# Turning the keys of a unit by 64x64 products with the identity, behind the values, in a two-layer decoder trunk on one core

## What is computed

```
def rwkv7_scan(r, w, k, v, kk, a):        # 16 heads of 64 channels
    def step(state, inp):
        rt, wt, kt, vt, kkt, at = inp
        sa = jnp.einsum("bhvk,bhk->bhv", state, -kkt)
        state = (state * wt[:, :, None, :] + sa[..., None] * (kkt * at)[:, :, None, :]
                 + vt[..., None] * kt[:, :, None, :])
        return state, jnp.einsum("bhvk,bhk->bhv", state, rt)
...
    xx = token_shift(h) - h
    xm = h[None] + xx[None] * mu.astype(F32)[:, None, None, :]
    rkvz = jnp.einsum("pbtd,pde->pbte", xm[:4], w_rkvz)
```

## Time and profile before

| | before |
|---|---|
| median of 3 runs | 3664.91 us |
| lowest, highest | 3661.26, 3670.25 us |
| the profiled execution | 3667.72 us |
| its span, first to last instruction | 3665.9 us |
| mean granted TensorE clock | 0.951 of full |
| TensorE busy | 3335.7 us, 91% |
| VectorE busy | 1609.7 us, 44% |
| ScalarE busy | 1316.8 us, 36% |
| GpSimd busy | 223.1 us, 6% |
| chain that ended last | TensorE 76%, VectorE 11%, DMA 5%, ScalarE 4% |

### The profile page before, as it was taken

The page is one execution under the profiler, slowest core; times in us unless marked ns, Lnnn a source line. Parts: engine busy times, 40 slices in busy tenths (PEclk is TensorE's granted clock), DMA queues, the critical chain, the costliest instruction groups (busy, mean ns, idle before and its releaser), DMA issues.

```text
span 3665.9 us, 76910 instructions
## 1 busy us (share of the span) xinstructions
PE 3335.7 (91%) x33546; PEld 2023.8 (55%) x33546; DVE 1609.7 (44%) x3443; ACT 1316.8 (36%) x2492; POOL 223.1 (6%) x345
## 2 busy tenths in 40 slices
PE   2898998899889858999999999999999999999998
PEld 1555465456446534666656466656556656556663
DVE  7254254335434534444554244454334454334442
ACT  0343243334333334333443233443324354323332
POOL 0010001010001000000000000000000000000000
PEclk8999999999999988999989999989999999999999
DMA  7231322223133121112011211111121111121111
GB/s 322 70 94 50 111 83 82 76 70 88 70 93 108 56 93 31 43 38 67 25 43 60 76 44 60 37 37 54 42 78 42 60 38 33 58 88 38 42 50 51
DMA packets 275847, 247.30 MB, mean 67 GB/s; under 512 B 16252, under 2 KB 251960, under 8 KB 272952
## 3 DMA queue, kind: packets, MB, share of 16 engines
q1 hardware_dynamic: 273208, 233.99, 20.2%
q0 software_dynamic: 2304, 8.39, 0.6%
HBM read 217.17 MB, written 25.18 MB: 66 GB/s over the span
## 4 chain that ended last, share of the span: by engine, by line
PE 76%; DVE 11%; DMA 5%; ACT 4%; issue 2%; SPq 1%; DVEq 0%; ACTq 0%; POOL 0%; another core or an unknown queue 0%
PE bank L655 20%; PE bank L529 14%; PE bank L624 6%; PE bank L739 4%; PE bank L752 4%; PE bank L562 3%; PE bank L748 3%; PE bank L526 3%; DVE xm L1534 3%; PE bank L604 3%; DVE arena L1595 2%; PE bank L666 2%; DMA xm<-in_ada_w 2%; PE bank L794 1%; DMA arena<-residual_scratch 1%
## 5 line engine op out<-in xcount | busy, mean ns | idle before, releaser
L655 PE MATMUL bank<-xm,wring 128*128 128x512 f32 x2048 | 947.8, 609 | 0.8 <-ACT arena L1083 0.8
L655 PEld LDWEIGHTS bank<-xm,wring 128*128 128x128 f32 x2048 | 386.5, 195 | 468.8 <-issue 457.6
L529 PE MATMUL bank<-arena,wring 128*128 128x512 f32 x1280 | 580.0, 593 | 13.4 <-ACT xm L948 5.1
L529 PEld LDWEIGHTS bank<-arena,wring 128*128 128x128 f32 x1280 | 231.0, 190 | 257.5 <-issue 246.0
L624 PE MATMUL bank<-wring,yT 128*128 128x512 f32 x776 | 346.6, 609 | 23.3 <-DVE yT L1427 10.1
L624 PEld LDWEIGHTS bank<-wring,yT 128*128 128x128 f32 x776 | 150.5, 195 | 216.4 <-issue 193.1
L1129 ACT COPY arena<-bank 128x256 f32<-128x256 f32 x256 | 96.4, 377 | 452.2 <-PE bank L752 452.2
L1802 POOL COPY r_Q<-ident 128x512 f32<-128x512 f32 x160 | 98.6, 616 | 2080.5 <-PE bank L752 2078.5
L1635 DVE COPY arena<-bank 128x64 f32<-128x64 f32 x256 | 57.5, 225 | 374.5 <-PE bank L784 369.6
L752 PE MATMUL bank<-arena,r_Q 64*64 64x32 f32 x5120 | 204.3, 223 | 0.0
L739 PE MATMUL bank<-arena 64*64 64x32 f32 x5120 | 196.4, 224 | 1.7 <-DVE arena L1619 1.0
(11 more groups left out here) (276 smaller groups left out, 5136.6 us busy)
## 6 DMA issues: line engine op xcount, KB each, us to landing
wring<-in_rw_w_rkvz SPq DMA_DIRECT2D x128, 512.0 KB, 4.4
wring<-in_ev_w_in SPq DMA_DIRECT2D x96, 512.0 KB, 5.3
xm<-in_ada_w SPq DMA_DIRECT2D x16, 1536.0 KB, 11.8
wring<-in_ev_w_out SPq DMA_DIRECT2D x32, 512.0 KB, 5.2
wring<-in_rw_w_out SPq DMA_DIRECT2D x32, 512.0 KB, 6.3
layer_input<-arena SPq DMA_DIRECT2D x4, 2052.0 KB, 7.6
wring<-layer_input SPq DMA_DIRECT2D x16, 513.0 KB, 6.8
xm<-in_x POOLq DMA_DIRECT2D x16, 512.0 KB, 5.4
```

Of the source, the lines that this page charges most:

```text
L529: mm = pe.matmul(pj[:, :], w[:, k, :], hT[:, k, 1:1 + TB], start=(k == 0), stop=(k == KC - 1))
L655: mm = pe.matmul(bank[1 if m == PROJ_Z else 0][:, :], w[:, k, :], xmv[MIX_OF[m]][:, k, :], start=(k == 0), stop=(k == KC - 1))
```

## The change

`turn_keys(v, 0)` and `turn_keys(v, 1)` become one call, right behind `turn_values(v)`. In place of 8 transposes of 128x128 it makes 32 products of 64x64 with ident64, four for each chunk: head h and half x of its 128 columns. Head 0 goes to MS, head 1 to UZ, each half x to its half of the partitions, so r_BKt has head 0 in its first 512 columns and head 1 in the second. The order within a chunk is (h, x) = (0, 0), (1, 1), (0, 1), (1, 0). The waits for MS and for ch_m both stand ahead of all products; ms_ready and bk_tr are posted by the last two. The projection between the two turns (3 steps) and behind them (2) becomes one run of 5. L790 and L802 read r_BKt by the new layout.

```diff
-            def turn_keys(v, x):
+            def turn_keys(v):
+
                 pe.wait_ge(S["r_arbk"], v + 1)
-                if x:
-                    pe.wait_ge(S["ch_m"], v * NCH)
-                else:
-                    pe.wait_ge(S["ms_free"], turn(BANKM, "bk", v))
-                for c in range(4):
-                    mm = pe.transpose((UZ if x else MS)[:, c * P:(c + 1) * P], r_BK[:, (4 * x + c) * P:(4 * x + c + 1) * P],
-                                      ident[:, :])
-                mm.then_inc(S["bk_tr"] if x else S["ms_ready"], 1)
+                pe.wait_ge(S["ms_free"], turn(BANKM, "bk", v))
+                pe.wait_ge(S["ch_m"], v * NCH)
+                for c in range(NCH):
+                    for h, x in ((0, 0), (1, 1), (0, 1), (1, 0)):
+                        r = half_of(h)
+                        mm = pe.matmul((UZ if h else MS)[half_of(x), c * RC:(c + 1) * RC],
+                                       r_BK[r, c * P + 64 * x:c * P + 64 * x + 64], ident64[r, :], start=True, stop=True)
+                        if c == NCH - 1 and h != x:
+                            mm.then_inc(S["bk_tr"] if h else S["ms_ready"], 1)
...
-                    pe.matmul(UZ[r, 0:64], r_BKt[r, c * P + 64 * h:c * P + 64 * h + 64], r_VT[r, cc], start=True, stop=False)
+                    pe.matmul(UZ[r, 0:64], r_BKt[r, 512 * h + c * RC:512 * h + (c + 1) * RC], r_VT[r, cc], start=True, stop=False)
...
-                    turn_keys(v, 0)
+                    turn_keys(v)
                     if v > RP and v % RP == 1:
-                        turn_keys(v, 1)
...
                     if inv:
-                        project(v + 1, PROJ_V, 0, 3)
-                    if not (v > RP and v % RP == 1):
-                        turn_keys(v, 1)
-                    if inv:
-                        project(v + 1, PROJ_V, 3, 5)
+                        project(v + 1, PROJ_V, 0, 5)
```

More of the change, by code:

```diff
@@ L801, in chunk @@
                 for h, r, s, g in heads:
-                    mm = pe.matmul(UZ[r, 0:64], r_BKt[s, c * P + 64 * h:c * P + 64 * h + 64], r_U[s, :], start=False, stop=True)
+                    mm = pe.matmul(UZ[r, 0:64], r_BKt[s, 512 * h + c * RC:512 * h + (c + 1) * RC], r_U[s, :], start=False, stop=True)
                 mm.then_inc(S["ch_z"], 1)
```

## The result

| | before | after |
|---|---|---|
| median | 3668.6 us (9 runs) | 3642.8 us (9 runs) |
| lowest, highest | 3661.3, 3673.7 | 3633.4, 3654.3 |
| ratio | | 0.993, 95% interval 0.9917 to 0.9943 |
| the profiled execution, its span | 3667.7, 3665.9 us | 3639.5, 3637.7 us |
| mean granted TensorE clock | 0.951 | 0.964 |

The change takes 26 us off; 3639 was forecast, in a range of 3622 to 3664. L numbers of the changed kernel differ from before by 1 to 3: on TensorE the keys are L705 (were L704), the scores L718 (L716), L773 is L771, L741 is L739, L796 is L794, and on VectorE the first operand is L1576 (L1579; L1575 or L1581 in some of the experiments), the mix L1531 (L1534), the masks L1592 (L1595), the state L1639 (L1642).

The account below looks back on a forecast made before the run. TensorE was taken to bound ordinary units, VectorE's queue the six mixing units. From the profiled 3667.7 us, +3 - 0.65 - 15.3 - 13 = -26 gave 3641.7, as a median 3639, range 3622 to 3664.

Parts of the forecast that it names:

- Part 1: Key turns on TensorE: 64 records in 0.93 us replace eight transposes; +0.1 us per unit, +3 over 28 units.
- Part 2: Waits for ch_m and MS right behind the values on TensorE: covered by the values, no cost.
- Part 3: VectorE gets r_BK some 2.55 us earlier: -15.3 us over six mixing units, -0.65 in the first unit.
- Part 4: TensorE's half clock behind idle times in the six mixing units: half avoided, -13 us, ends 0 and -26.5.
- (a): Rival on the key turns: quadrants don't overlap for long, keys take 1.87 us; 3671, no change; chance 0.12.
- (b): Rival on the key turns: each quadrant-pair change costs a slow 0.11 us step; slower, 3697; chance 0.06.
- (c): Rival on VectorE's early start: masks wait for something else, only the turns' cost counts; 3668; chance 0.10.
- (d): Within the forecast: clock in the six units never falls, 3626, or always, 3652; forecast with it has chance 0.72.

Follow-up runs that it names:

- the run with two quadrants: The changed kernel with all (0,0) and (1,1) products first, then all (0,1) and (1,0): 3677.2 us, ratio 1.0032 to before.
- place alone: The kernel of before with both calls of its 128x128 transposes right behind the values, no 64x64 products: 3639.8 us, ratio 0.9929.
- products alone: The changed kernel with its 64x64 products cut in two calls, the second behind three projection steps as before: 3683.8 us, ratio 1.0039.
- second profile of the same kernel: The changed kernel, nothing altered, profiled again on another chip: median 3650.9 us, ratio 0.9948, span 3652.5 us.
- the Z mix moved: The changed kernel with VectorE's part of the Z mix behind the first quarter, not ahead of the masks: 3630.0 us, ratio 0.99; again 3623.3, ratio 0.988.

## Why the prediction was right, point by point

- **Part 1, the turns.** Forecast 0.93 us for the keys, +0.1 per ordinary unit, projection 2.0 us after the values begin, scores at 9.05, unit length 57.5. Measured 57.54, 1.99 and 9.05, the +0.1 exactly, and its reason too: 0.10 on the first projection record, seen behind both turns where the products stand apart. The choice between four records and two per 0.058 us was the largest in the sum, 0.93 against 1.87; the eight records of rows 5 gave the right one, and the run with two quadrants showed the other. The Trainium skill's rule in "TensorE: Matmul & The Clock Gate" (section "Part 3: Packing small matmuls — row/col tiling"), by which weight loads overlap products only where the row group differs, doesn't hold for these quadrants: (0, 0) and (0, 1) share one, and with all four in turn the keys take 1.14 us, with two at a time 1.79. The least distance of about 25 ns between starts, from the same page of the Trainium skill (section "Wait — 56ns, not 53.3ns?"), would make 1.6 us for 64 records, an estimate; the trace has 1.14 with the change of tile size.
- **Missing in part 1** were the small stalls: the 17 ordinary units gave +3.8 where 1.7 was due (the sum over the shortest unit is 2.7 us, and was 0.7).
- **Part 2, the waits.** VectorE's state update ends at 1906.86, 0.56 us after the values begin, and the keys start at 0.85 behind them: no wait, as said. TensorE's idle time behind ScalarE's copies in the three units with an output projection is 5.7 us and was 5.3, and elsewhere it is no longer than before.
- **Part 3, r_BK earlier.** Forecast 2.36 us after the values begin; measured 2.33, in K units 3.03 and not the 2.36 of "all units", since the keys wait 0.47 for MS there; they waited 0.51 before, which is why the masks still came 2.5 us earlier. In Z units they came 2.6 us earlier, and the idle time before L771 fell from 3.38 to 0.67 (0.8 forecast). The first unit's L794 came 0.74 earlier; the unit gained 1.5, of which 0.65 was forecast; the rest is not explained. The two runs that part place and products show that this is the cause: place alone 0.9929, products alone 1.0039.
- **Part 4, the clock.** Forecast: half of the half clock avoided, 13 us, beside 15.3 by VectorE's start. In the first profile K and Z units gained 24.0 together, where 28.3 was forecast. TensorE's idle time in them fell from 32.9 to 21.7 us, so 11.2 of the 24.0 was waiting and 12.8 the clock. The waiting came out smaller than 15.3 because of what is late next: before L771 16.3 us went, but 4.7 came back before L794, which TensorE now reaches ahead of VectorE in each of the six (0.8 to 1.2 us of idle time), as the 32 records of L739 ahead of it take 1.12 us at full clock where they took 1.92 at half. The half is right in count in that profile: all three K units kept the full clock at the start (1.00 from 1854.0 to 1858.0) and all three Z units fell to half, for 3.4 us less each (10.2 in place of 13.7 in the one shown). That the size came so close, 12.8 against 13, is luck. The half was a middle value between two ends, not worked out, and in the second profile of the same kernel two of the three K units fell at the start too. Even where they kept it, half clock came back behind their V mix, for 10.2, 10.2 and 6.8 us. The 86.5 us that the term starts from are the lengths of six stretches; at half clock in them were 82. In the Z units all of it could have been had: with the Z mix moved, they take 57.5.
- **Luck in the sum.** The forecast of 3641.7 for the profiled execution met 3639.5; the second profile of the same kernel, on another chip, was 3654.3. Another 4.3 us of the first profile's gain lie ahead of the K units (4.2 in one, 76.4 to 72.2), where no mix stands before the masks and the forecast has nothing; in either kernel such units take 72 to 74 us or 76 to 77. The medians, 3642.8 against 3668.6 and 3650.9 against 3670.6, give 26 and 20 us, where 26 was forecast.
- **The rivals.** (a) and (b) fell with the 1.14 us. (c) fell with the masks at 12.26. Of (d) neither end came: over the two profiles of the changed kernel four of six K units and none of six Z units kept the full clock at the start.

What the prediction didn't say, though its sum holds both terms, is that the change's own two parts pull against each other: the place carries the gain, and transposes at that place are better than the products, by 3 us in the ordinary units in every pair of profiles.

## What to carry to other kernels

When a step is moved and rebuilt at once, price the place and the build apart: here a buffer given back 2.6 us earlier was the gain, and the new products a small loss. Before moving the producer, look at what stands between the buffer and the consumer in the other engine's program; moving a 5.4 us step that nobody is waiting for out of that queue brought as much, and both together (with transposes) brought 60 us, 3610.8 against 3670.6 on one chip. A price read from eight records held over 64, because they had the same shape and the same mixture of quadrants.

## What the runs showed of the hardware that was not expected

- Products of 64x64 in fp32 that alternate over all four quadrants go through at four records per 0.058 us, for 64 records on end; confined to two quadrants at a time the same 64 take 1.79 us in place of 1.14.
- Small tiles inside a run of 512-column products cost 0.09 us going in, 0.15 coming out and 0.10 on the first large record, each time; transposes of 128x128 there cost 0.44 us for four and nothing on the record behind them.
- The same idle time isn't always followed by the same clock. In K units TensorE idles 0.62 us before L741 and 0.83 before L796, with short products between: behind that the clock was full in the three of the first profile of the changed kernel, and half in two of the three of its second. With 0.6 to 0.7 us more ahead of these (before L773), in the Z units, it was half in all six.
- Small stalls of TensorE mostly come 2.3 to 2.9 us behind the start of a DMA packet of the kind "instruction": 43 of 57 do, where one moment in twelve has such a packet at that distance.
